# Three modulation vectors ahead of the attention, and three pairs of PSUM banks in turn for the q, k and v units

## The reference

```python
# silu(c) @ w_mod + b_mod gives six vectors of 1024 for each of two layers
for i in range(2):
    sh1, sc1, g1, sh2, sc2, g2 = adaln_params(c[:, None, :], w_mod[i], b_mod[i])
    hx = modulate(x, sh1, sc1)
    if i == 0:                                   # differential attention
        hc = modulate(h_ctx, csh1, csc1)         # 256 context positions
        k_c, v_c = project_kv(hc, w_qkv)
        q_l = apply_rope(project_q(hx, w_qkv))
        k_l, v_l = project_kv(hx, w_qkv); k_l = apply_rope(k_l)
        y = diff_head_out(latent_diff_attention(q_l, [k_c, k_l], [v_c, v_l], lam), ...)
    else:
        y = multiscale_pool(hx, pool_w, pool_scale)
    x = layer_norm(ALPHA * x + g1 * y, ...)
    x = layer_norm(ALPHA * x + g2 * swiglu(modulate(x, sh2, sc2), w_in, w_out), ...)
```

## Time and profile before

| | |
|---|---|
| median of 3 runs | 1218.4 us (1217.55 to 1225.79) |
| profiled execution, its own time | 1219.3 us |
| its span, first to last instruction | 1217.6 us |
| granted TensorE clock, mean | 0.976 |
| PE busy | 1147.6 us (94% of the span) |
| VectorE (DVE) busy | 771.1 us (63%) |
| ScalarE (ACT) busy | 570.6 us (47%) |
| GpSimd (POOL) busy | 62.3 us (5%) |
| DMA, mean | 194 GB/s |

### The profile page before, as it was taken

The page is one execution under the profiler, slowest core; times in us unless marked ns, Lnnn a source line. Parts: engine busy times, 40 slices in busy tenths (PEclk is TensorE's granted clock), DMA queues, the critical chain, the costliest instruction groups (busy, mean ns, idle before and its releaser), DMA issues.

```text
span 1217.6 us, 15382 instructions
## 1 busy us (share of the span) xinstructions
PE 1147.6 (94%) x6348; PEld 963.3 (79%) x6348; DVE 771.1 (63%) x868; ACT 570.6 (47%) x783; POOL 62.3 (5%) x119
## 2 busy tenths in 40 slices
PE   4899979899999996999999899999989999999998
PEld 2677756679998885899988677876877789998886
DVE  1686668578787978885544754546656467665444
ACT  2542327555444333544443556645765355554342
POOL 2011120000111101010000000000000000000000
PEclk8999989999999997999999989999999899999999
DMA  9965680147999874785554598877633255555540
GB/s 310 382 232 211 230 294 30 52 139 251 330 319 326 298 250 140 263 279 173 175 192 128 132 187 168 171 157 153 144 134 127 86 200 175 176 191 188 179 175 35
DMA packets 119431, 236.80 MB, mean 194 GB/s; under 512 B 5569, under 2 KB 60162, under 8 KB 119234
## 3 DMA queue, kind: packets, MB, share of 16 engines
q1 hardware_dynamic: 105314, 185.74, 50.8%
q0 software_dynamic: 14048, 50.09, 11.7%
HBM read 234.75 MB, written 1.05 MB: 194 GB/s over the span
## 4 chain that ended last, share of the span: by engine, by line
PE 83%; DVE 7%; DMA 3%; ACT 3%; issue 2%; SPq 2%; DVEq 0%; ACTq 0%
PE ps L1751 17%; PE ps L1752 17%; PE ps L1753 17%; PE ps L1790 7%; PE ps L1789 7%; PE ps L1788 7%; PE ps L1880 3%; PE ps L2016 1%; PE ps L2029 1%; DVE modraw L1104 1%; DMA mod<-in_w_mod 1%; DMA raw<-in_w_in 1%; DVE wL L1016 1%; PE ps L1930 1%; DVE rt L1162 1%
## 5 line engine op out<-in xcount | busy, mean ns | idle before, releaser
L1016 DVE TENSOR_TENSOR wL<-raw,wH 128x1024 fp32r<-128x1024 f32 x328 | 397.7, 1222 | 298.6 <-ACT wH L571 297.3
L571 ACT ACTIVATE wH<-raw 128x1024 fp32r<-128x1024 f32 x328 | 343.1, 1057 | 406.4 <-PE ps L1753 260.6
L1751 PE MATMUL ps<-wH,aH 128*128 128x512 f32 (+1 forms) x624 | 253.6, 406 | 18.4 <-DVE aL L1044 9.7
L1752 PE MATMUL ps<-wL,aH 128*128 128x512 f32 (+1 forms) x624 | 246.8, 396 | 0.0
L1753 PE MATMUL ps<-wH,aL 128*128 128x512 f32 (+1 forms) x624 | 246.5, 395 | 0.0
L1788 PE MATMUL ps<-aH,wH 128*128 128x256 f32 x768 | 219.0, 285 | 0.0
L1790 PE MATMUL ps<-aH,wL 128*128 128x256 f32 x768 | 217.4, 283 | 0.0
L1789 PE MATMUL ps<-aL,wH 128*128 128x256 f32 x768 | 217.3, 283 | 0.0
L1751 PEld LDWEIGHTS ps<-wH,aH 128*128 128x128 f32 x624 | 120.8, 194 | 52.9 <-issue 23.3
L1788 PEld LDWEIGHTS ps<-aH,wH 128*128 128x128 f32 x768 | 147.4, 192 | 0.7 <-issue 0.7
L1789 PEld LDWEIGHTS ps<-aL,wH 128*128 128x128 f32 x768 | 147.4, 192 | 0.7 <-issue 0.7
(11 more groups left out here) (306 smaller groups left out, 1261.4 us busy)
## 6 DMA issues: line engine op xcount, KB each, us to landing
raw<-in_ffn_w_in SPq DMA_DIRECT2D x88, 512.0 KB
modraw<-in_w_mod POOLq DMA_DIRECT2D x80, 512.0 KB, 5.9
raw<-in_w_in SPq DMA_DIRECT2D x32, 1024.0 KB
raw<-in_ffn_w_out SPq DMA_DIRECT2D x22, 1024.0 KB
raw<-in_w_up SPq DMA_DIRECT2D x16, 1024.0 KB
raw<-in_w_down SPq DMA_DIRECT2D x16, 1024.0 KB
mod<-in_w_mod SPq DMA_DIRECT2D x8, 1024.0 KB, 12.0
raw<-in_attn_w_qkv SPq DMA_DIRECT2D x8, 1024.0 KB
```

Of the source, the lines that this page charges most:

```text
L571: nc.scalar.activation(wH[:, n % WS, :], raw[:, (n // 2) % RAW, (n % 2) * 1024:(n % 2) * 1024 + 1024], ACT.Copy).then_inc(w_hi, 1)
L1016: V.tensor_tensor(wL[:, n % WL, :], raw[:, (n // 2) % RAW, (n % 2) * 1024:(n % 2) * 1024 + 1024], wH[:, n % WS, :].bitcast(fp32), ALU.subt ...
L1751: T.matmul(outp, xh, h, start=first, stop=False)
L1752: T.matmul(outp, xh, l, start=False, stop=False)
```

## The change

- **Vectors.** `IN_QKV` goes from 4 to 3: vectors (0,2), (0,3), (0,4) are worked out in the projections and the attention's start, (0,5) in the first feed-forward. Steps in chunks 2 to 5 are 7, 7, 8, 2 (before 6, 6, 10, 10); totals stand at (3,1) and (5,1), puts at (3,2) and (5,2). The first three accumulate in `g2b0` and not in `modraw`; g2b0's bias is loaded after step 24. Three steps go to the attention's end, the feed-forward has steps from chunk 1 on (before: from chunk 3), and totals behind chunks 3, 6, 8 and at k = 1 and 8 of out0.
- **Banks.** Units q0 to v3 use pairs 0-1, 2-3 and 6-7 by a table, and wait by a second table. `rotate` counts a latent unit as emptied after its four products; a new semaphore `rot_done` marks its end. The second k chunk's emptying order: k1 before k0.
- **Order.** x is loaded in four column quarters, one behind each block of mod0. In the start ScalarE's second weight copy stands behind the high part of x, VectorE's first behind `mod_put`. `low_ctx(0)` stands before q0's rotation. `heads` stand after sub-chunks 1 and 2. POOL's thirteen small loads for later stages move from the start to behind step 24. `scores(0)` and `scores(1)` wait for v1 and v2 emptied and for the put of vector 1.

```diff
-VECS = [(0, 2), (0, 5), (0, 3), (0, 4), (1, 0), (1, 1), (1, 2), (1, 3), (1, 4), (1, 5)]
+VECS = [(0, 2), (0, 3), (0, 4), (0, 5), (1, 0), (1, 1), (1, 2), (1, 3), (1, 4), (1, 5)]
...
+IN_QKV, IN_FF0, IN_FF1 = 3, 9, 10
+QKV_STEPS = {(c, j): ((2, 2, 2, 1), (2, 2, 2, 1), (2, 2, 2, 2), (1, 1, 0, 0))[c - 2][j] for c in range(2, 6) for j in range(4)}
+QKV_SELECT = {(3, 1): 0, (5, 1): 1}
+QKV_PUT = {(3, 2): 0, (5, 2): 1}
+QKV_BANK = (0, 2, 6, 0, 2, 0, 6, 2, 0, 6)
+QKV_FREE = (0, 0, 0, 1, 2, 3, 4, 5, 6, 7)
+TOTAL_BANK = {1: 4, 8: 2}
+FF0_SELECT = {3: 3, 6: 4, 8: 5}
+FF0_PUT = {4: 3, 7: 4, 9: 5}
...
-            b = 2 * (un % 2)
+            if un < UNITS["att"]:
+                b = QKV_BANK[un]
+            else:
+                b = 2 * ((un + (un < UNITS["wo"])) % 2)
...
-                if m == 0:
-                    sp.dma_start(x[:, :, :], a["x"].rearrange("b (t p) d -> p (b t) d", p=P)).then_inc(x_in, 16)
+                cols = slice(256 * m, 256 * m + 256)
+                sp.dma_start(x[:, :, cols], a["x"].rearrange("b (t p) d -> p (b t) d", p=P)[:, :, cols]).then_inc(x_in[m], 16)
...
                         if k == MT - 1 and v <= IN_FF0 - 1:
                             pool.wait_ge(vec_sum, v)
-                        elif v <= IN_QKV and n - MT < KT * IN_QKV:
-                            pool.wait_ge(vec_step, n - MT + 2)
                         else:
                             pool.wait_ge(vec_step, n - MT + 1)
...
+            for v in range(1, IN_QKV):
+                vec_load(v)
+            pool.wait_ge(vec_step, KT * IN_QKV)
+            pool.dma_start(g2b0[:, :], a["b_mod"][0:1, 5 * D:6 * D].to_broadcast([P, D])).then_inc(bias0_in, 16)
...
                 mod_copy(c)
-                for j in range(2):
-                    adv(2 * c + j)
+                adv(2 * c)
                 act.wait_ge(mod_out, c + 1)
                 hi(GROUPS["x"] + c, aH[:, 2 * c:2 * c + 2, :], mod=mc(c))
+                adv(2 * c + 1)
...
-                    link(ins)
+                    ins.then_inc(acc_out, 1)
+                    dve.wait_ge(acc_out, freed[0])
...
-                    ins.then_inc(acc_out, 1)
+                    ins.then_inc(rot_done, 1)
...
-            adv(8)
-            adv(9)
+            for j in range(8, 11):
+                adv(j)
+            low_ctx(0)
             rotate(UNITS["q"], n + 7, False)
...
+                if c == 2:
+                    rotate(UNITS["k"] + 1, summed("k", 0), False)
+                    rotate(UNITS["k"], summed("k", 0), True)
+                elif c == 3:
+                    rotate(UNITS["k"] + 2, summed("k", 2), True)
+                    rotate(UNITS["k"] + 3, summed("k", 2), False)
...
-                if r in (6, 10, 14):
+                if r in (6, 10):
                     square_sum((r - 6) // 4)
-                elif r == 12:
+                elif r == 14:
                     normed(0)
+                elif r == 15:
+                    square_sum(2)
...
             normed(1)
+            vec_steps(3)
...
-                        if c >= 3:
+                        if c >= 1:
                             vec_steps(1)
...
-                            at_least(pe, acc_out, un - 1)
+                            at_least(pe, acc_out, QKV_FREE[un] if un < UNITS["att"] else un - 1)
+                            if un == UNITS["k"]:
+                                pe.wait_ge(mod_out, NMOD0)
+                            elif un == UNITS["v"]:
+                                pe.wait_ge(mod_out, NMOD0 + 1)
...
+                    if (c, sub) == (3, 1):
+                        pe.wait_ge(acc_out, 4)
                     if (c, sub) in QKV_SELECT:
                         vec_total(QKV_SELECT[c, sub])
+                    elif (c, sub) == (2, 2):
+                        heads(1)
+                    elif c in (3, 4) and sub in (1, 2):
+                        heads(2 * c - 5 + sub)
...
-                    pe.wait_ge(acc_out, un - 1)
+                    pe.wait_ge(acc_out, UNITS["v"] + 2 + r)
...
+            pe.wait_ge(mod_out, NMOD0 + 2)
             scores(0)
             scores(1)
...
-                    if layer == 0 and k == 10:
-                        vec_total(7)
+                    if layer == 0 and k in (1, 8):
+                        vec_total({1: 6, 8: 7}[k])
```

More of the change, by code:

```diff
@@ L353, in vec_acc @@
         def vec_acc(v):
-            return (psb if v >= IN_FF0 else g2b1)[:, :]
+            return (g2b0 if v < IN_QKV else g2b1 if v < IN_FF0 else psb)[:, :]
         def vec_row(v):
@@ L456, in _ @@
             nc.gpsimd.memset(cT[:, :, :], 0.0).then_inc(cT_zero, 1)
[L460 to L474, removed]
             def vec_load(v):
@@ L507, in _ @@
             pool.dma_start(g1b[:, :], a["b_mod"][0:1, 2 * D:3 * D].to_broadcast([P, D])).then_inc(bias0_in, 16)
-            pool.dma_start(g2b0[:, :], a["b_mod"][0:1, 5 * D:6 * D].to_broadcast([P, D])).then_inc(bias0_in, 16)
             for v in range(1, IN_QKV):
                 vec_load(v)
+            pool.wait_ge(vec_step, KT * IN_QKV)
+            pool.dma_start(g2b0[:, :], a["b_mod"][0:1, 5 * D:6 * D].to_broadcast([P, D])).then_inc(bias0_in, 16)
+            for j, nm in enumerate(("norm_mix_2", "norm_mlp_2", "norm_ple_2")):
+                pool.dma_start(rows2[8 * j:8 * j + 8, :], a[nm].rearrange("l (r p) -> (l r) p", p=P))\
+                    .then_inc(rows2_in, 16)
+            pool.dma_start(rows2[24:32, :], a["gla_out_norm_2"].rearrange("l h (r p) -> (l h r) p", p=P)).then_inc(rows2_in, 16)
+            pool.dma_start(rows2[32:33, :], a["moba_k_norm_2"]).then_inc(rows2_in, 16)
+            pool.dma_start(rows2[33:34, :], a["moba_q_norm_2"]).then_inc(rows2_in, 16)
+            for j in range(6):
+                w = (a["ln_g"], a["ln_b"])[j % 2]
+                k = (0, 2, 3)[j // 2]
+                pool.dma_start(rows2[34 + 8 * j:42 + 8 * j, :],
+                               w[k // 2, k % 2:k % 2 + 1, :].rearrange("l (r p) -> (l r) p", p=P)).then_inc(rows2_in, 16)
+            with nc.allow_non_contiguous_dma(reason="16 columns of w_in"):
+                pool.dma_start(lrw[:, :, :], a["w_in_2"][0].rearrange("(k p) n -> p k n", p=P)[:, :, LR0:LR0 + GRANK])\
+                    .then_inc(lrw_in, 16)
             ln_load(0)
@@ L673, in _ @@
                         heads_out(0)
+                    elif (c, j) == (2, 2):
+                        heads_out(1)
+                    elif c in (3, 4) and j >= 1:
+                        heads_out(c - 1, (2 * j - 2, 2 * j - 1))
                 if c == 4:
@@ L1090, in vec_steps @@
                     tile = modraw[:, n % MT, :]
-                    if n < KT * IN_QKV:
-                        total, before = tile, modraw[:, (n - 1) % MT, :]
-                    else:
-                        before = vec_acc(n // KT)
-                        total = vec_row(n // KT) if k == KT - 1 else before
+                    before = vec_acc(n // KT)
+                    total = vec_row(n // KT) if k == KT - 1 else before
                     if k == 0:
@@ L1184, in _ @@
             n = SUBS["qkv"]
-            adv(8)
-            adv(9)
+            for j in range(8, 11):
+                adv(j)
+            low_ctx(0)
             rotate(UNITS["q"], n + 7, False)
-            adv(10)
-            low_ctx(0)
+            low_ctx(1)
+            adv(11)
             rotate(UNITS["q"] + 1, n + 8, False)
-            adv(11)
-            for j in range(1, 4):
+            for j in range(2, 4):
                 low_ctx(j)
@@ L1925, in vec_total @@
                     for k in range(KT):
-                        ins = T.matmul(ps[:, 2 if v == IN_FF0 - 1 else 7, 2 * k:2 * k + 2], row[:, k * P:(k + 1) * P], cst[:, C_ONE:C_ONE + 2],
+                        ins = T.matmul(ps[:, TOTAL_BANK.get(v, 7), 2 * k:2 * k + 2], row[:, k * P:(k + 1) * P], cst[:, C_ONE:C_ONE + 2],
                                        start=True, stop=True)
@@ L1961, in _ @@
             mod_select(0)
-            pe.wait_ge(x_in, 16)
             x_group(0)
@@ L1981, in heads @@
             def heads(unit):
-                pe.wait_ge(acc_out, UNITS["q"] + unit + 1)
+                if unit in (2, 4):
+                    pe.wait_ge(acc_out, {2: 4, 4: 5}[unit])
+                else:
+                    pe.wait_ge(rot_done, {0: 1, 1: 2, 3: 3, 5: 4}[unit])
                 g = GROUPS["q"] + 2 * unit
```

56 lines of the change are left out of this document (20 added, 36 removed).

## The result

The changed kernel takes 1203.46 us in the median of four executions (1199.1 to 1204.5), the kernel before beside it 1217.97. The medians are 14.5 us apart; the ratio is 0.9856 (0.9821 to 0.9890). The profiled execution took 1199.1 us, the fastest of its four, with a span of 1197.4; that of after2 had a span of 1201.5.

What follows compares the result with a forecast made beforehand. TensorE, busy 94% of the span, was taken as the bound, so only removing its waits or work pays. 1.2 + 9.5 - 0.3 + 0 + 1.4 - 0.2 = 11.6 us gave 1206.8 us, range 1203.5 to 1212.5.

Steps and rivals of the forecast that it cites:

- The start: Loading before the projections: 1.2 us gained (0.7 to 1.7), 0.7 from block 3 landing earlier, 0.5 from moved small transfers.
- The split: At the start, x in four column quarters lets modulation block 3 land earlier: 0.7 us gained.
- The new copy order: At the start, reordered first copies bring the first projection forward about one copy each, but block 3 swallows that.
- The projections: Four projection chunks: TensorE's waits go, 9.5 us gained (8.2 to 9.9), less 0.3 for k3 waiting for k1's products.
- The door: From projections to first exponential: 6.9 us instead of 8.3, 1.4 gained; scores(0) now waits for vector 1's put.
- The attention: Attention rounds: moved work and three added steps fit into existing waits, cost 0; at most 3.6 us without that cover.
- First feed-forward and down projection: Feed-forward: tighter hand-offs at units 3 and 6, 0.2 us lost; in out0, one step fewer at its end, 0.
- quick landing: Rival at the door: load 19 lands in 4.0 to 4.5 us, start saves 1.7; gain 13 to 14, 1205.0 us; chance 0.17.
- no wait took the place of the banks: Rival in the projections: VectorE takes the banks' place, about half of 8.2 us stays; 1211.5 us; chance 0.15.
- the third pair's totals never held TensorE: Rival in the projections: totals sharing banks 6 and 7 become the waits, 2 to 3 us lost; 1209.5; chance 0.08.
- the split was not slow: Rival at the start: x's quarters run at half the rate, 1.2 becomes -1.7; 1209.7 us; chance 0.04.
- at the door no more than 5.6 us passed: Slower rival: landings of 10.3 us delay fourth-slot hand-offs at door and feed-forward; 1219.7, decisive from about 9.8; chance 0.04.

Runs made afterwards that it cites:

- after2: The changed kernel timed and traced once more, no edit: 1202.4 us against 1220.8 for the kernel before, ratio 0.9858.
- xwhole: The changed kernel with x loaded in one transfer behind block 0 instead of four quarters: 1201.0 us, ratio 0.9843.
- banks: The changed kernel with two pairs of banks up to the attention instead of three: 1213.5 us, ratio 0.9946.
- door2: The changed kernel with the total of (0,3) two sub-chunks earlier, behind (4,3), and its put at (5,0): 1203.5 us, ratio 0.9861.
- fill: door2 plus 18 matmuls that nobody reads between scores(1) and scores(2): 1200.8 us, ratio 0.9845.
- bfill: The kernel before plus unread matmuls in two stops, 24 between scores(1) and scores(2) and 8 ahead of the last scores: ratio 0.9984.
- before2: The kernel before run once more without edit for a second trace: a single execution of 1218.2 us.
- bfill2: bfill timed and traced once more, against the kernel before: ratio 0.9994; its traced execution took 1213.7 us, its median was 1218.3.
- late: door2 with scores(0) made to wait for the last weight copy: a single execution of 1200.0 us.
- start: The changed kernel with x in one transfer, small POOL loads early and the old order of first copies: a single execution of 1204.7 us.

## Why the prediction was right or wrong

**The start** (1.2 us): K came 3.8 us earlier, 3.4 in the mean of the seven traces with the new start and three pairs; less the 2.2 for low_ctx that is 1.2 to 1.6. The size was right for wrong reasons. The split, 0.7 of it, was worth nothing that can be seen (xwhole). The new copy order, which block 3 was to swallow, brought, with the small transfers gone, the first projection 0.6 to 2.0 us nearer to the select: block 3 had not been waited for in either trace of before. It landed at 42.2 and 41.8, and TensorE came for it at 42.39 and 42.73. In the changed kernel's first trace it landed at 40.8 and TensorE waited 0.11 us for it: there it was just in time.

**The projections** (9.5, less 0.3 for k3): banks has 9.4, and stage by stage it is 11.1 + 2.2 (low_ctx) - 1.9 (the total that left) - 1.6 (next sentence) = 9.8; k3's wait was 0.3 as worked out. The slow stretch behind the total of (0,3), which I left as it was, recurred in no trace of a changed kernel: 1.6 us more. What stopped it was not tested.

**The door** (+1.4): VectorE's gap and the put as predicted; I put the first exponential near 164, it came at 164.55. From the first scores to the first maxima 2.2 us passed at 1.2 GHz (161.11 to 163.29) where I wrote 1 to 2. The stage P-X itself is 0.8 us longer than before and not 1.4 shorter: TensorE ended the projections 1.6 us sooner than my count, for want of the slow stretch, and as I had written, the exponentials do not notice that. Counted with it, the door gave 0.8. Up to here the sum said 13.7 us with the total of (0,5) counted as gone; the traces have 14.1.

**The attention** ("Cost 0"): **this step failed.** The traces have 4.4 us of gain, 2.4 from the first exponential to T and 2.0 to L. I priced the door by the first exponential alone. I had used a fall of the clock in the chunk of the earlier trace rows, behind a total's small matmuls, but not at the door, where the earlier trace rows shows scores 2 taking 2.08 us behind 6.62 us of idleness. The change moves that stop ahead of scores 0 and 1; door2 and fill show the same 2.6 us lost and won, bfill shows it without the change. With two pairs of banks (banks) the moved stop gave only 1.1 us of it. For the second part, the fall behind the 2.48 us stop of the last rounds occurs in before, before2, door2 and fill, and not in seven other traces with the same stop; I found no rule for it.

**First feed-forward and down projection** (-0.2, and -1.9 for the total that moves there): the hand-offs at units 3 and 6 cost TensorE nothing, as figured. "One step fewer stands at its end: 0" was wrong in size: the total of vector 7 waits 1.51 us, where before that of vector 6 waited 0.79 and that of 7 not at all. Stage by stage -2.1 us in the first trace, as the sum had it, and -5.3 in the second, where the clock fell behind the 1.51 us.

**Behind the pooling**, where nothing is changed, the two traces gained 2.8 us. The stage has 752.5 to 757.5 us over all fourteen traces and 752.6 to 757.5 in the four of the kernel before, so I do not count this as the change's. Its length follows the clock: TensorE's idle time in it is 20.8 to 22.4 us in all fourteen, while the time at 1.2 GHz is 24.7 us in the shortest but one (bfill2) and 41.4 in the longest (bfill), with a correlation of 0.94 between that time and the length.

The low end of my range was not worked out soundly: quick landing with a start of 1.7 gives 11.6 + 1.3 + 0.5 = 13.4 us, the 1205.0 of the rival itself, and not 1203.5.

None of the rivals held: no wait took the place of the banks, the third pair's totals never held TensorE, the split was not slow, at the door no more than 5.6 us passed from POOL's issues (144.53) to step 20. The gain above my sum has its largest part in the traces in the attention's clock: 4.4 us, with 0.4 up to the first exponential and 2.8 behind the pooling, less 1.6 between (17.6 against 11.6). How much of the timings' excess, 2.9 us in the first comparison and 5.7 in the second, that clock makes is not shown: the same 4.4 us given to the kernel before bought 0.7 to 2.0.

## What to carry to other kernels

Follow a change stage by stage to the point where the next stop lies, and price the work behind each stop at the level of the clock that it will find: here stops of 4.4 and 5.6 us ahead of the first scores cost 1.0 and 0.8 us (late and the changed kernel against door2), while one of 5.0 us ahead of the rounds, in which each step waits for the last, slowed these by 2.6. The third pair of banks was worth about the sum of the waits for the evacuation of the other two, and that sum could be read before. A gain ahead of a stretch whose loads keep the DMA at over 0.9 may be taken back there, as in bfill2. Where a stop can't be removed, matmuls that nobody reads may pay, but time them: the kernel before gained 4.4 us by them in two stages of its trace and 0.7 to 2.0 in its time.

## What the runs showed of the hardware

The same stop of 2.48 us was followed by the 1.2 GHz level in four traces of eleven, and one of 1.51 us in two traces of eight (after2 and banks), but not in the changed kernel's other trace. With eight unread matmuls in the 2.48 us stop, in three traces, it never was. The time of identical code behind the pooling varied by 5 us between traces, along with the time at 1.2 GHz (24.7 to 41.4 us). The kernel before waited for the modulation blocks after the first 0.98 us in one trace, 0.06 in the second, 0.8 and 2.5 in bfill and 1.73 in bfill2; in the ten traces of the changed kernel and its variants, start among them, no such wait was over 0.11.
